# One block from the output projection to the experts, and an expert block's input rows gathered on the tensor engine with a one-hot matrix

## What is computed

```python
h = layer_norm(alpha * x + mix @ w_out, ln1_g, ln1_b)           # 512 x 1024
g_logits = h @ rg_w + rg_b                                      # 4 groups
e_logits = h @ re_w + re_b                                      # 16 experts in layer 0, 32 in layers 1 and 2
group    = argmax(softmax(g_logits))                            # one group for each token
e1, e2   = the two best experts of that group
weights  = g_p * (e_p / sum(e_p))
y        = for each expert e and each of its tokens: (silu(h @ w_gate[e]) * (h @ w_up[e])) @ w_down[e]
out      = layer_norm(alpha * h + weights-weighted sum of a token's two y, ln2_g, ln2_b)
```

## Time and profile before

| | us |
|---|---|
| median of 3 runs | 3034.09 (3024.65 to 3036.26) |
| the profiled execution | 3027.6, with a span of 3025.9 from the first to the last instruction |
| PE busy, of the span | 2245.3 (74%) |
| DVE, ACT, POOL busy | 928.1, 467.7, 521.0 |
| moved by DMA | 647.09 MB, mean 214 GB/s |

### The profile page before, as it was taken

One profiled execution on the slowest core, in us unless ns is written; L12 is line 12 of the kernel. 1 busy time (PEld: TensorE's weight loads), 2 busy tenths in 40 slices (PEclk: granted clock), 3 DMA queues, 4 the chain that ended last, 5 costly groups with the idle time before them and its releaser, 6 DMA issues. The chain is left out here.

```text
span 3025.9 us, 80584 instructions
## 1 busy us (share of the span) xinstructions
PE 2245.3 (74%) x34278; PEld 1535.2 (51%) x34279; DVE 928.1 (31%) x2250; ACT 467.7 (15%) x1058; POOL 521.0 (17%) x915
## 2 busy tenths in 40 slices
PE   8987885878499867787556529988887857667852
PEld 3436654756344644565434314457884445455631
DVE  0214532222500753222111162036667322111214
ACT  1024300111100510110000111023331000000100
POOL 0000104322300001332111120011113132122212
PEclk9988997999699987899777759989997959789976
DMA  5212127998412004999999841000003259999994
GB/s 223 84 58 105 37 106 258 401 412 337 168 56 84 29 17 163 346 404 411 415 412 414 328 168 34 22 1 3 3 3 135 67 204 409 414 410 406 409 415 181
DMA packets 108264, 647.09 MB, mean 214 GB/s; under 512 B 30610, under 2 KB 52370, under 8 KB 74340
## 3 DMA queue, kind: packets, MB, share of 16 engines
q1 hardware_dynamic: 41440, 567.30, 46.4%
q0 software_dynamic: 30336, 55.02, 5.4%
q10 hardware_dynamic: 36356, 22.86, 2.5%
HBM read 599.98 MB, written 45.09 MB: 213 GB/s over the span
## 5 line engine op out<-in xcount | busy, mean ns | idle before, releaser
L1162 PE MATMUL ps<-ring,arena 128*32 128x128 f32 x13440 | 444.9, 295 | 222.8 <-DMA ring<-in_experts 104.3
L1162 PEld LDWEIGHTS ps<-ring,arena 128*32 128x32 f32 x13440 | 408.5, 120 | 273.1 <-issue 150.2
L1129 POOL DMA_DIRECT2D arena<-xybuf x640 | 317.5, 497 | 989.1 <-DVE arena L1210 902.3
L1171 PE MATMUL ps<-ring,arena 128*32 128x256 f32 x3360 | 250.1, 433 | 101.8 <-DMA ring<-in_experts 71.7
L1222 DVE TENSOR_TENSOR arena<-arena,ps 128x64 f32<-128x64 f32 x296 | 65.6, 222 | 673.4 <-ACT arena L1200 673.4
L1200 ACT ACTIVATE arena<-ps 128x64 f32<-128x64 f32 x296 | 66.1, 223 | 1202.6 <-PE ps L1162 1014.1
L1162 PE MATMUL ps<-arena 128*32 128x128 f32 x5504 | 179.8, 292 | 68.3 <-DMA arena<-in_experts 51.6
L1171 PEld LDWEIGHTS ps<-ring,arena 128*32 128x32 f32 x3360 | 107.9, 121 | 208.2 <-DMA ring<-in_experts 82.0
L1162 PEld LDWEIGHTS ps<-arena 128*32 128x32 f32 x5504 | 164.6, 118 | 92.7 <-DMA arena<-in_experts 63.0
L1232 DVE COPY arena<-ps 128x256 f32<-128x256 f32 x148 | 62.8, 425 | 360.3 <-PE ps L1171 231.6
L355 PE MATMUL ps<-ring,arena 128*128 128x512 f32 x384 | 166.0, 593 | 3.1 <-PEq L192 3.1
(11 more groups left out here) (371 smaller groups left out, 3000.9 us busy)
## 6 DMA issues: line engine op xcount, KB each, us to landing
ring<-in_experts SPq DMA_DIRECT2D x165, 2048.0 KB, 32.7
arena<-in_experts SPq DMA_DIRECT2D x50, 2048.0 KB, 32.7
xt_mem<-in_experts SPq DMA_DIRECT2D x25, 2048.0 KB, 37.6
ring<-in_mixer_chunks SPq DMA_DIRECT2D x24, 2048.0 KB, 12.8
xybuf<-arena ACTq DMA_DIRECT2D x640, 32.0 KB, 9.8
arena<-xybuf POOLq DMA_DIRECT2D x640, 32.0 KB, 6.6
xybuf<-arena SPq DMA_DIRECT2D x1, 9216.0 KB, 25.5
rows<-in_ln_g POOLq DMA_DIRECT2D x6, 512.0 KB, 5.3
```

The lines of the kernel that those rows point to most:

```text
L1129: pool.dma_start(x_in[at, b, :], xybuf[bass.ds(start, BLK), q * W:(q + 1) * W]).then_inc(s_loaded[b], 16)
L1162: ins = pe.matmul(ps[at, 2 + half, 0:P], xg[:, k, :], w_gu[half][:, k, q, :], start=(k == 0), stop=(k == NK - 1))
L1171: ins = pe.matmul(ps[at, 4, 0:W], hT[:, f, :], w_d[:, f, q * W:(q + 1) * W], start=(f == 0), stop=(f == NT - 1))
```

## The change

The two blocks of the head and the expert loop's block become one, `project_and_experts`. In it:

- The router works on rows that are not normed. PE turns a tile as soon as the residual is added and multiplies it with router weights scaled by the norm's gain (`weighted`); mean and deviation are put in afterwards by DVE (`finish_logits`), with column sums of the weights that PE forms once. Three of the four tiles are turned, and two logit groups formed, ahead of the last projection's end; ACT, not DVE, applies mean and deviation to the rows (`normed`), and DVE the gain and bias (`scale_rows`).
- Ranks within an expert come from two products (`ones` and `before` with all of `pick`) and a few sums on DVE. `y_sb` is cleared by POOL.
- Scatter, its wait and all loads of input rows are gone. DVE makes a one-hot matrix (128 token partitions by 4 tiles by 32 rows) for the next block (`hot`), and PE multiplies it with `x_tok` into PSUM bank 5 (`gather`, 16 matmuls of 256 columns, once for each block). DVE turns the result out of PSUM into `xg`.
- PE runs `gather(g + 1)` between gate/up and down of block g.
- SP loads the third expert's weights when the last logits are done.

In the RWKV stage some semaphores are shared with counts in place of separate ones; its work and order stay. The core of the diff:

```diff
+                    dve.wait_ge(loaded.sem, l0 + 64)
+                    dve.wait_ge(router_in.sem, 16 * router_loads(l))
+                    for n, col in enumerate((g_col, b_col)):
+                        link(dve.tensor_tensor(weighted[n], wr, bc(col, R_PAD), ALU.mult))
+                        ins = dve.tensor_reduce(col_sums[:, n, :], weighted[n].rearrange("p k r -> p r k"), AX, ALU.add)
+                    for j in range(NT):
+                        add_rows(j)
+                        scales(j)
+                        if j < NT - 1:
+                            scale_rows(j)
+                        if j == NT - 1:
+                            for n in range(NT):
+                                finish_logits(n)
...
+                            ins.then_inc(mm.sem, 1)
+                            if j >= 1 and c == 0:
+                                turn(j - 1, 0)
+                                turn(j - 1, 1)
+                        if j >= 1 and j < NT - 1:
+                            raw_logits(j - 1)
+                            if j == 1:
+                                sums()
+                    turn(NT - 1, 0)
+                    raw_logits(NT - 2)
+                    turn(NT - 1, 1)
+                    raw_logits(NT - 1)
+
+                    pe.wait_ge(*at_step("picked", 1))
+                    pe.matmul(ps[:, 3, 0:NT * E], ones, pick.rearrange("p j e -> p (j e)"), start=True, stop=True)\
+                      .then_inc(steps["counted"].sem, 1)
+                    pe.matmul(ps[:, 1, 0:NT * E], before, pick.rearrange("p j e -> p (j e)"), start=True, stop=True)\
+                      .then_inc(steps["counted"].sem, 1)
+
+                    def gather(n):
+                        pe.wait_ge(s_hot, n + 1)
+                        for j in range(NT):
+                            for q, to in enumerate(quarters):
+                                ins = pe.matmul(ps[to, 5, 0:W], one_hot[:, j, :], x_tok[:, j, q * W:(q + 1) * W],
+                                                start=(j == 0), stop=(j == NT - 1))
+                        ins.then_inc(s_gathered, 1)
...
                                 ins.then_inc(s_gu[half], 1)
+                            gather(g + 1)
                             pe.wait_ge(*there[2])
                             pe.wait_ge(s_y, g + 1)
...
-                    for j in range(NT):
-                        for n in range(2):
-                            pool.indirect_dma_start(out=xybuf, out_offset=bass.IndirectOffsetOnAxis(ap=slots_i[:, n, j:j + 1], axis=0),
-                                                    in_=x_tok[:, j, :], in_offset=None).then_inc(s_sent, 16)
-                    pool.wait_ge(s_sent, 2 * NT * 16)
-                    def load_quarters(start, b):
-                        for q, at in enumerate(quarters):
-                            pool.dma_start(x_in[at, b, :], xybuf[bass.ds(start, BLK), q * W:(q + 1) * W]).then_inc(s_loaded[b], 16)
...
+                    def hot(n, count):
+                        if n != 0:
+                            dve.tensor_scalar(ahead_by, ahead_by, -float(BLK), None, ALU.add).then_inc(s_steps, 1)
+                            dve.wait_ge(s_steps, count)
+                        dve.tensor_tensor(one_hots.rearrange("p n j s -> p (n j) s"),
+                                          bc(ahead_by.rearrange("p n j -> p (n j)"), BLK), mid(iota_f, 2 * NT), ALU.is_equal)\
+                           .then_inc(s_steps, 1)
+                        dve.wait_ge(s_steps, count + 1)
+                        dve.tensor_tensor(one_hot, one_hots[:, 0, :, :], one_hots[:, 1, :, :], ALU.add).then_inc(s_hot, 1)
...
                             dve.wait_ge(s_gu[1], g + 1)
-                            dve.wait_ge(s_loaded[after], p * 64 + 64 + 64 * (b == AHEAD - 1))
-                            take_inputs(after)
+                            dve.wait_ge(s_gathered, g + 2)
+                            take_inputs()
+                            hot(2, 2 * g + 4)
                             dve.wait_ge(s_down, g + 1)
```

More of the change, by code:

```diff
@@ L317, in load_router @@
                     load(brow[:, 4:NR], a["moe_re_b_2"][l - 1].unsqueeze(0))
[L319 to L348, removed]
-                    for j in range(NT):
[L350 to L380, removed]
-                            dve.wait_ge(mm.sem, m0 + 2 * j + c + 1)
-                            xc = x_tok[:, j, c * CH:(c + 1) * CH]
-                            ins = dve.scalar_tensor_tensor(xc, xc, alpha, ps[:, 2 * j + c, :],
-                                                           ALU.mult, ALU.add)
-                        link(ins)
-                        if j == 0:
-                            dve.wait_ge(loaded.sem, l0 + 32)
-                    norm_tiles(dve, link, update, n0)
@@ L1087, in moe_stage @@
             HALF = P // 2
+            first = moe_at[l] - 2
+            m0, l0, n0 = mm.take(2 * NT), loaded.take(64), {"stat": stat.take(NT), "sq": sq.take(NT)}
+            for c in range(2):
+                used[first + c] = (mm.sem, m0 + 2 * NT - 1 + c)
             def value(eng, n, low=1, high=MAXB):
@@ L1093, in _ @@
                 def _(sp):
+                    stream_mixer(sp, first + SLOTS, first + SLOTS + 2)
+                    sp.wait_ge(*at_step("logits_done", NT))
+                    for kind in range(3):
+                        sp.dma_start(third_at[kind], expert_src(l, 2, kind)).then_inc(arrived_x[kind].sem, 16)
+                    sp.wait_ge(*at_step("placed", TABLED))
                     def load(e, q, kind):
@@ L1141, in _, with turn @@
+                    pool.memset(y_sb, 0.0).then_inc(steps["places_ready"].sem, 1)
                 @block.tensor
                 def _(pe):
+                    NR_, wr, brow = router_at(l)
+                    def turn(j, c):
+                        pe.wait_ge(*at_step("rows_added", 2 * j + c + 1))
+                        for k in range(4):
+                            to = (4 * c + k) * P
+                            ins = pe.transpose(ps[:, 2 * j + c, k * P:(k + 1) * P], x_tok[:, j, to:to + P], ident)
+                        ins.then_inc(steps["rows_turned"].sem, 1)
@@ new lines, in raw_logits @@
+                    def raw_logits(j):
+                        if j == 0:
+                            pe.wait_ge(*at_step("router_weighted", 1))
+                        for k in range(NK):
+                            if k % 4 == 0:
+                                pe.wait_ge(*at_step("rows_taken", 2 * j + 2))
+                            ins = pe.matmul(ps[:, 2 * j, 0:R_PAD], xT[:, k, j * P:(j + 1) * P], weighted[0][:, k, :],
+                                            start=(k == 0), stop=(k == NK - 1))
+                        ins.then_inc(steps["logits"].sem, 1)
@@ L1173, in expert @@
                             ins.then_inc(s_down, 1)
+                    pe.wait_ge(*at_step("placed", LAST_TILE_SCALED))
+                    gather(0)
+                    pe.wait_ge(*at_step("placed", TABLED))
                     with pe.Fori(0, E // 3) as i:
```

342 lines of the change are left out of this document (192 added, 150 removed).

## The result

The kernel after takes 2914.73 us (median; 2912.01 to 2916.9), the kernel before 3030.93 in the same group of runs: a ratio of 0.9617, with a 95% interval of 0.9594 to 0.964. The forecast was 2960 with a range of 2918 to 2998. The question behind the experiments is where these 45 us come from. Not all of them lie in the kernel: the sum of the forecast stood for the profiled execution (2954), and 6 us were added to it because that execution was faster than the median of its kernel. The profiled execution of after took 2915.37, 0.6 over its own median.

A forecast was written before the change was run, and what follows sets the result against it. No single bound: layer 0's loop by PE, layers 1 and 2 by weight loads, with PE doing little in the heads. -91.8 + 30 + 2 - 14 = -73.8 us from 3027.6 gives 2954, as a median 2960; range 2918 to 2998.

The forecast's parts named there:

- The heads: Last projection to first gate/up: 24 + 5.7 us replaces 61.6 in layer 1; three layers save 91.8 us.
- an allowance for registers: Head: 1.2 us for loop registers that PE loads behind the table, taking the path from 22.8 to 24 us.
- The gather on PE: Expert loop: 1.70 us per gather at full clock, a tight block going from 5.44 to 6.89 us.
- The rival at 2996: Gather of 2.2 us by the skill page's packing, or PE partly at the lower clock; sum -38 us; chance 12%.
- Layer 0's loop: PE-bound expert loop of 43 block steps: +30 us, bounds +15 and +45.
- the stores' waits: Layer 0's loop: 33 us in which y's copy waits for old stores, expected not to come on top.
- Layers 1 and 2: Weight-bound expert loops: removed loads give -19 us each; net +2 in layer 1 and -14 in layer 2.
- the dense run: Layer 1, 16 blocks of five experts: PE needs 116 us, engines 83, so engines stand idle 18 us.
- The first (2925): Gather nearly free in dense runs, or stores free more DMA: layer 0 +10, layer 1 -12 us; chance 12%.
- The heads gave the whole amount, not half: Rival: DVE's chain as long as the old two, or late loads, so heads give -46 us: 3006; chance 8%.
- The slower case: Gather at the lower clock through the loops, 3.4 us a block: +63 us, 3097; chance 4%.
- the 2.7 of the forecast: Expert loops: at about 2.7 us a gather the change turns from a gain to a loss.

The follow-up runs named there:

- the head alone: Kernel after with the one-block head, but scatters and block loads on POOL as in the kernel before, no one-hot matrix or gather: 2987.49 us, ratio 0.9855.
- the loads put back: Kernel after, gather kept, with POOL's four input-row DMAs per block restored in layers 1 and 2 into an area nothing reads: 2987.09 us.
- one DMA for a block in place of four: Kernel after, POOL again loading each block's 128 KB in layers 1 and 2, as one DMA of 32 rows of 4 KB: 2989.29 us.
- the run that gathers once: Kernel after with the gather left out of the loop on PE, every block working on the first block's rows: 2824.79 us.

## Why the prediction was right, and where it failed

**The heads** were right step by step. The timeline of layer 1's head in after, which answers the earlier trace rows:

```profile
1168.62 0.69 DVE L1159 SCALAR_TENSOR_TENSOR x_tok<-x_tok,ps 128x512 f32<-128x512 f32 x1 [1.99 <-PE ps L1035]
...
1180.21 0.79 PE L1051 MATMUL ps<-arena,cst 128*128 128x128 f32 x2 [5.97 <-DVE arena L1234]
...
1182.54 0.28 DVE L1240 TENSOR_REDUCE arena<-ps 128x32 f32<-128x128 f32 x1
...
1187.16 3.64 PE L1061 MATMUL ps<-x_tok,arena 128*32 128x256 f32 x32 [5.73 <-DVE arena L1198]
...
1190.85 0.45 DVE L1271 STREAM_TRANSPOSE arena<-ps 128x256 f32<-128x256 f32 x1 [1.72 <-PE ps L1061]
...
1191.45 0.74 PE L1084 MATMUL ps<-ring,arena 128*32 128x128 f32 x12 [0.65 <-DVE arena L1271]
```

From the addition at 1168.62, PE starts on the pick after 11.6 us (11.8 in the forecast), DVE on the counts after 13.9 (14.3), PE on the first gather after 18.5 (18.6), and gate/up after 22.8 (22.8, or 24 with an allowance for registers that wasn't needed). The work put ahead of it on PE is 6.3 us (5.7).

**The gather on PE** was right. Two tight blocks of layer 1, which answer (there 5.44 us apart):

```profile
1246.36 3.68 PE L1084 MATMUL ps<-ring,arena 128*32 128x128 f32 x128
1249.85 1.91 PE L1061 MATMUL ps<-x_tok,arena 128*32 128x256 f32 x32
1251.58 1.91 PE L1094 MATMUL ps<-ring,arena 128*32 128x256 f32 x32
1253.31 2.92 PE L1084 MATMUL ps<-ring,arena 128*32 128x128 f32 x100
```

A block is 1253.31 - 1246.36 = 6.95 us (6.89 in the forecast) and a gather 1.73 (1.70). The rival at 2996 wanted 2.2 us, and it falls. That 2.2 was an estimate from the fourfold packing of the Trainium skill ("TensorE: Matmul & The Clock Gate", Measured speedup vs the span model), which the trace doesn't bear out. It divided by the packing's loss a time that had been measured on packed matmuls; no run here has this form unpacked, so the page's speedups themselves aren't tested.

**Layer 0's loop** came out at +26.2 for +30. 43 x 6.95 + 15 x 1.15 + 5 is 321, the measured loop. As forecast, the waits for old stores are gone and the stores land sooner: 6.1 us where the earlier trace rows had 24.9.

```profile
DVE arena L1295 <- PE ps L1094: 20.3, 44, 0.5
...
xybuf<-arena ACTq DMA_DIRECT2D x78, 32.0 KB, 6.1
```

The experiments divide the net otherwise than I did: about -23 for the loads and +49 for the gather (321.0 against 271.6), where the sum had -33 for the stores' waits and +64 for the gather. Both parts were too large, and their errors met: that the net fits within 4 us is partly luck.

**Layers 1 and 2: one term was mis-sized.** I took the price of an expert's weights, 15.2 us, from the earlier trace rows and left it as it was when the loads went. The loads' removal was put at their own packets, -19 us in each layer, and both lower bounds (-15 for layer 1, -19 for layer 2) leave room for no more. This is the step that failed. By the same working in after, from the queue's row over 1460 to 1600 us, it is 0.979 x 140 / 58.61 x 6.29 = 14.7:

```profile
q1 hardware_dynamic: 4025, 58.61, 97.9%
```

That is 15.1 us in layer 1's loop and 14.1 in layer 2's. The rest of these terms stands: in layer 2 the other parts changed by -21.4 + 0.7 + 6.2 = -14.5 (forecast -14); in layer 1 by -20.9 + 1.1 + 25.9 = +6.1 (forecast +2, with 21 us of idle engines of which the dense run was to make 18). The dense run does show idle engines now, a share of 0.84 where the earlier trace rows had 1.02:

```profile
1216.00:1345.00 129.00, 124.92 (x3438) 100.03 (x3434) 45.26 (x158) 14.45 (x41) 0.00 (x0) 1.00 0.84 345
```

**Layer 1's exit was missing from the sum**, 9.5 us. The kernel before, POOL's last loads, the end of ACT's waits, and the first gathering of results:

```profile
1716.73 1.65 POOL L1129 DMA_DIRECT2D arena<-xybuf  x3 [0.15 <-issue]
...
1727.22 0.20 ACT L1205 ACTIVATE small<-cst 128x1 f32<-128x1 f32 x1 [7.21 <-DMA xybuf<-arena]
...
1735.93 1.00 POOL L1257 DMA_INDIRECT arena<-xybuf,arena  x1 [17.55 <-POOLq L1091]
```

After:

```profile
1684.13 0.20 ACT L1148 ACTIVATE small<-cst 128x1 f32<-128x1 f32 x1 [6.83 <-DMA xybuf<-arena]
...
1685.27 1.03 POOL L1320 DMA_INDIRECT arena<-xybuf,arena  x1 [515.36 <-POOLq L951]
```

ACT's wait for its last stores is alike, about 7 us; before, 8 us more pass until the block opens, and POOL is the engine that came to it 17.55 us after its last issue, though a load lands within 8.5. The layers' last blocks decide how late that issue is. The loads cause it: the exit is 14.1 with the head alone, 10.7 with the loads put back, 5.6 with one DMA for a block in place of four, and 4.8 in the kernel before without them. What POOL does between the landing and the block's end, the trace doesn't show, and it stays open. An exit can be long without loads, too: in the run that gathers once, layer 1's is 9.3 us, but there ACT waited longer for its last stores, behind which weights were still arriving, and the block opened 0.3 us later:

```profile
1611.10 0.20 ACT L1147 ACTIVATE small<-cst 128x1 f32<-128x1 f32 x1 [9.92 <-DMA xybuf<-arena]
1611.58 2.95 ACT L1328 ACTIVATE x_tok<-x_tok 128x1024 f32<-128x1024 f32 x3 [0.27 <-PEq L951]
```

**The range** was missed by 3 us. Had either of these two terms been in the sum, forecast and range would have lain some 10 us lower or more and the time inside; the 6 us from the profiled execution to the median alone would have done it too, and they say nothing of the change. So how near the edge the time fell is chance. The two terms, 29 us of weights' packets and 9.5 of an exit, are not.

**The rivals.** The first (2925) came closest in time but not in its mechanism: it wanted +10 in layer 0, where +26 was measured. The heads gave the whole amount, not half. The slower case needed a gather at the lower clock level through the loops; the granted clock share of layer 2's loop rose from 0.85 to 0.94, and most gathers took the full clock's price. At the lower level (granted share 0.50) were the first gathers of the heads of layers 1 and 2, 3.64 us each; seven of the 104 in these layers' loops were partly there (0.53 to 0.71) and took 2.6 to 3.5 us. With two gathers a block, 3.46 us, the kernel is 1.2% slower than before, so a gather at that price would indeed lose. A straight line from one gather (1.73 us, 2914.7) to two (3066.1) crosses 3031 at 3.1 us, not at the 2.7 of the forecast, since the loads' removal pays more than I had put in. It is an estimate: the cost isn't straight, as layer 2 shows (1.7 us for the first gather, 27.3 for the second).

## What to carry to other kernels

Where the DMA engines bound a loop, the price of a second stream of loads is not the share of its own packets: read the main stream's time per byte with and without it, and open the bound of the estimate to at least that. A price read from a stretch that holds the disturbance is not a constant once the disturbance is removed. And look at what an engine off the path owes at the end of its block: prefetches that nobody uses can hold the barrier.

## What the runs showed of the hardware

- In layer 2's loop, loads of 6.9 MB on POOL's queue beside 182.5 MB of weights in 16 KB packets cost 29 to 34 us in place of their own 19 to 21: the weights' packets go from 617 to 635 to 643 ns. In layer 1's loop, which had 22 us to spare, it was 23 to 26. It happens from POOL's and from ACT's queue, with packets of 2 and 4 KB on POOL's, and whatever array is read; at half the bytes it is 623 ns. Only some of the packets are lengthened: about as many as there are packets of loads of 2 or 4 KB. What the two streams of loads share isn't shown.
- The mean of a packet rises without a second stream of loads as well, when the stream has pauses: in layer 0's loop of after it is 638 ns, because 3% of the packets take over 1000 ns, most of them within 3 us behind a pause of over 1 us; the others take 613. So means are to be compared between dense streams.
- 5.4 MB of stores less, by contrast, left the weights' packets at 619 ns.
- The same 1 KB row pieces are more packets on ACT's queue than on POOL's: 20159 - 9888 = 10271 for 7.0 MB against 6688 for 6.9 MB, and their time is 0.090 x 527.6 - 0.043 x 499.2 = 26.0 us against 20.5.
- More work on PE came with a higher granted clock: 0.85 to 0.94 to 0.99 in layer 2's loop with none, one and two gathers for each block.
